# Two first-weight cells loaded whole, and the first ring load of the experts in four pieces

## The chip, the cores and the metric

The kernel runs on one core of one Trainium2 chip. The metric is the device time of one execution in microseconds. The profiled execution also gives a span, from the first to the last instruction of the program. The engines are PE (TensorE matmuls; PEld are its weight loads), DVE (VectorE), ACT (ScalarE), POOL (GpSimd) and SP (SyncE, which here only issues DMA transfers and waits; "SPq" in the rows). L927 means line 927 of the kernel before.

## The reference, cut to what matters

Two transformer-like blocks run one after the other on x of shape (1, 256, 1024) in float32. The first has two kinds of attention and a gated feed-forward layer. The second has a retention branch, an RWKV-7 recurrence and a mixture of 32 experts, of which each token uses two:

```
def second_block(x, ...):
        ret = retention(...) ; rw = rwkv7_time_mix(...)
        h = h + concat([ret, rw]) @ w_out
        h = h + hier_moe(rms_norm_2(h, norm2_gain), ...)
    return rms_norm_2(h, final_norm_gain)
...
    def expert_block(args):
        xblk, e = args
        hdn = jax.nn.silu(xblk @ w_gate[e]) * (xblk @ w_up[e])
        return hdn @ w_down[e]
```

Each expert has three matrices (gate, up, down) of 2 MB, so the 32 experts are 192 MB (201 million bytes) of weights, each of which is read once.

## The kernel before, in words

**Order of the work.** The first block runs up to about 345 us, then the projections of the second block, the recurrence (roughly 480 to 530 us), its output projection (to 554 us), the router (to 563 us) and the experts to the end. TensorE's program is written out by hand up to the first group of experts; after that it is a loop.

**Experts.** The experts are taken in eight groups of four (EG = 4). A group's work is: gather the chosen tokens (line 1942), multiply by gate and up (line 1962: for m in gate, up; for half in 0, 1; for k in 0..3; for expert j in 0..3), silu and product, multiply by down (line 1990), scatter. Up to 32 tokens of an expert make 32 columns, and the four experts run side by side on TensorE. After the last k of a half, the matmul of each expert adds 1 to the semaphore pieces_read, so the sync queue knows which weights may be overwritten.

**The ring.** From the second group on, the weights go through eight slots of 2 MB (two places with four experts each) in the big SBUF tensor arena. load_set (line 913) waits for pieces_read and issues the 2 MB load of one expert's matrix into slot_of(place, j); its landing adds 16 to ring_in[place][j], for which TensorE waits.

**The first group's weights** cannot go through the ring: they are put, before the ring starts, wherever room comes free. There are 24 cells of 1 MB, each one half of a matrix, that is 2048 columns of 128 rows. The table CELL says which half (q = 0, 1 gate; 2, 3 up; 4, 5 down) of which expert lies in which place: (0..3, i) are pieces of arena, (NQ, 0) and (NQ, 1) lie in the spent constants cst, (NQ + 1, 0) in x, (NQ + 2, i) in smaller pieces of several tensors. first_load (line 927) issues a cell, in pieces if first_parts says so, each piece after the fill for which it is told to wait: a cell in the tuple SPACED goes as four quarters of 512 columns (256 KB), the others go whole. The fills are TensorE's results in PSUM, named by tuples: ("U", c, par), ("St", c) and ("Y", ...) are steps of the recurrence over four chunks c of 64 tokens. All loads of lines 927 and 913 are on the one queue of SP, in the order in which moe_stream writes them: an issue that waits holds up all that stand behind it. The matmuls of the recurrence that appear in the rows are lines 1671 (U), 1688 (U with the state), 1705 (St), 1715 and 1732 (Y).

**Around the change.** In the recurrence moe_stream issues (2, 2) in quarters, (NQ, 1) in quarters waiting for ("U",1,1), ("St",1), ("St",1), ("U",2,1), (3, 2) in quarters waiting for ("U",2,1), ("St",2), ("St",2), ("U",3,1), and then the third piece of (NQ + 2, 3). The last first cell is (NQ + 1, 0), into x, issued at 561.58. The first ring load is expert 6's gate matrix into slot_of(1, 2). That slot is the same memory as the cells (3, 0) and (3, 1), which hold the first half of gate for experts 2 and 3; its columns 0 to 2047 are the one and 2048 to 4095 the other. It goes out once pieces_read is 4, that is when the first half of the first group's gate has been multiplied. The next ring load waits for pieces_read 5, one expert into the second half.

Of the kernel before, what the change touches and what calls it, by code (L numbers as in the profile page):

```python
# [30 lines left out]
P = 128  # L31
# [26 lines left out]
EG = 4  # L58
# [10 lines left out]
NQ = 4  # L69
# [260 lines left out]
def build(nc, A, out):  # L330
# [13 lines left out]
    with ExitStack() as ctx:  # L344
# [3 lines left out]
        def sem(name):  # L348
            return ctx.enter_context(nc.semaphore(name))
# [144 lines left out]
        def slot_of(place, j):  # L494
            lo = 2 * QUAD * place + SLOT * j
            return arena[:, lo:lo + SLOT]
# [103 lines left out]
        pieces_read = sem("pieces_read")  # L600
# [3 lines left out]
        u_first = sem("u_first")  # L604
        y_first = sem("y_first")
        rows_spent = sem("rows_spent")
        y_squared = sem("y_squared")
        y_gained = sem("y_gained")
        centre_ready = sem("centre_ready")
# [11 lines left out]
        ring_in = [[sem(f"ring_in{n}_{j}") for j in range(EG)] for n in range(2)]  # L621
# [31 lines left out]
        for u in range(9):  # L653
            lo = 512 * u if u < 4 else (2048 if u == 4 else NQKV + 512 * (u - 5))
            n = 256 if u == 4 else 512
# [193 lines left out]
        moe_w = {"gate": A["w_gate_2"], "up": A["w_up_2"], "down": A["w_down_2"]}  # L849
# [1 line left out]
        ALLQ = NG * QUADS_PER_GROUP  # L851


        SPACED = ((2, 0), (2, 1), (2, 2), (NQ, 0), (NQ, 1), (3, 3), (3, 2))

        SETS = 2 * 3
        LAST = NG // 2 - 1
# [26 lines left out]
        def _(sp):  # L884
# [19 lines left out]
            def load_set(r, pair, s, read, js=range(EG)):  # L904

                gp, kind = s // 3, ("gate", "up", "down")[s % 3]
                e0 = pair * (2 * EG) + gp * EG
                w = moe_w[kind][e0:e0 + EG] if isinstance(e0, int) else moe_w[kind][bass.ds(e0, EG)]
                w = w.rearrange("j (p k) n -> p j (k n)", p=P)
                for j in js:  # L910
                    if read is not None:
                        sp.wait_ge(pieces_read, read[j] if isinstance(read, dict) else read + (j + 1))
                    nc.sync.dma_start(slot_of(s % 2, j), w[:, j, :]).then_inc(ring_in[s % 2][j], 16)
# [6 lines left out]
            def first_load(at, j, *steps, lo=0, hi=4):  # L920

                w, col = half_of(*held_in[at, j]), 0
                for n, part in enumerate(first_parts(at, j)):
                    if lo <= n < hi:
                        if steps:
                            wait_filled(sp, *steps[n])
                        nc.sync.dma_start(part, w[:, col:col + part.shape[1]]).then_inc(quad_in[at][j], 16)  # L927
                    col += part.shape[1]

            def moe_stream(r, first):  # L930
                if first:
# [8 lines left out]
                    first_load(3, 3, *inv(("G1", 0), ("G1", 1), ("G2", 0), ("G2", 1)))  # L940
                    sp.wait_ge(mixed_ready, 1)
                    first_load(2, 2, ("U", 0, 1), ("St", 0), ("St", 0), ("U", 1, 1))
                    first_load(NQ, 1, ("U", 1, 1), ("St", 1), ("St", 1), ("U", 2, 1))
                    first_load(3, 2, ("U", 2, 1), ("St", 2), ("St", 2), ("U", 3, 1))
                    first_load(NQ + 2, 3, lo=2, hi=3)
                    sp.wait_ge(mixed_ready, NT)
                    sp.wait_ge(u_first, NCH - 1)
# [24 lines left out]
                    sp.wait_ge(xn_ready, 2 * NT)  # L972
                    sp.wait_ge(scattered, 2 * NT)
                    first_load(NQ + 1, 0)
                    load_set(0, 0, 3, {2: 4, 0: 5}, (2, 0))
                    sp.wait_ge(pieces_read, 8 + 1)
                    nc.sync.dma_start(quad[EXTRA_AT[0]][EXTRA_AT[1]], half_of(*EXTRA)).then_inc(extra_in, 16)
                    load_set(0, 0, 3, {1: 6, 3: 12}, (1, 3))
# [86 lines left out]
        def _(pe):  # L1065
# [841 lines left out]
            def moe_group(r, pair, gp, final=False):  # L1907
# [41 lines left out]
                for m in range(2):  # L1949
                    for half in range(2):  # L1950
                        if m == 0 and half == 1:
                            if isinstance(n, int) and n == 0:
                                wait_emptied(pe, "count")
                            gather(2)
                            gather(3)
                        for k in range(4):
                            if m == 0 and (half, k) in GATHERED_AT:
                                pe.wait_ge(xg_ready, len(GATHERS) * n + GATHERED_AT.index((half, k)) + 1)
                            for j in range(EG):
                                if k == 0:  # L1960
                                    half_ready(m, half, j)
                                ins = mm(psum[32 * j:32 * j + 32, MB[4 + m], :], xg[:, 4 * half + k, 32 * j:32 * j + 32],  # L1962
                                         weights(m, half, j, 512 * k), start=half == 0 and k == 0,
                                         stop=half == 1 and k == 3, skip_group_check=True)
                                if k == 3:
                                    ins.then_inc(pieces_read, 1)
                pe.wait_ge(shares_ready, n + 1)
# [56 lines left out]
            def moe_round(r):  # L2024
                if isinstance(r, int):
                    moe_group(r, 0, 0)
                    pe.wait_ge(count_ready, 1)
                    rows_most.append(pe.value_load(cnt[0:1, 0:1], min_val=0, max_val=T))
                    with pe.Fori(0, NG // 2 - 1) as pair:
                        moe_group(r, pair, 1)  # L2030
                        moe_group(r, pair + 1, 0)
                else:
                    with pe.Fori(0, NG // 2) as pair:
                        for gp in range(2):
                            moe_group(r, pair, gp)
# [1196 lines left out]
```

## Time and profile before

| | us |
|---|---|
| median of 3 runs | 1003.07 |
| lowest, highest | 1001.17, 1004.86 |
| the profiled execution | 1002.88 |
| its span | 1001.1 |
| PE busy, of the span | 873.7 |
| PEld, DVE, ACT busy | 603.4, 449.5, 331.9 |
| all DMA: moved, mean rate | 294.35 MB, 294 GB/s |

The page cuts the span into 40 slices of 25 us and gives the busy share of each engine in tenths (9 is 90% or more), the share of the 16 DMA engines, and the rate. The chain of waits follows the last instruction back to what released it, step by step. "issue" is time in which an engine waited for nothing that the profile shows. A DMA row gives the size of one transfer and the time from its issue to its landing.

### The profile page before, as it was taken

What the parts mean: (1) busy time and instruction counts of PE and PEld (TensorE: products, weight loads), DVE (VectorE), ACT (ScalarE), POOL (GpSimd) and SP (SyncE); (2) the same over time, 40 slices, a digit from 0 to 9 for tenths busy, and PEclk for the clock granted to TensorE, in tenths of its full rate; (3) what the DMA queues carried; (4) which work ended last, traced back from release to release, by engine and by line L of the source; (5) the groups of instructions that cost most, each with busy time, mean ns of one, the idle gap of its engine ahead of it and who ended that gap; (6) DMA issues with size and microseconds to landing.
All of it is one profiled execution on the core that took longest, in us unless ns stands there. A gap on an engine that the chain in (4) does not pass through costs nothing.

```text
span 1001.1 us, 16180 instructions
## 1 busy us (share of the span) xinstructions
PE 873.7 (87%) x6998; PEld 603.4 (60%) x6998; DVE 449.5 (45%) x586; ACT 331.9 (33%) x433; POOL 22.0 (2%) x35
## 2 busy tenths in 40 slices
PE   9999999999999999999989987767858776785785
PEld 8889988888888889989879632211312221131223
DVE  6776878688877438898766311000100000010002
ACT  6466664565555318745523300000000000000002
POOL 0420000000000000000100000000000000000000
PEclk9999999999999999999999999888977877788889
DMA  9893425576654536362459999999999999999995
GB/s 317 258 349 136 156 86 168 169 248 195 208 186 169 210 132 240 111 221 98 124 164 388 387 419 420 429 427 428 429 428 428 428 427 429 429 429 429 423 425 215
DMA packets 76113, 294.35 MB, mean 294 GB/s; under 512 B 5263, under 2 KB 32671, under 8 KB 62736
## 3 DMA queue, kind: packets, MB, share of 16 engines
q1 hardware_dynamic: 70496, 283.91, 72.6%
q10 hardware_dynamic: 4128, 6.34, 1.8%
q0 software_dynamic: 1424, 3.16, 1.1%
q8 instruction: 50, 0.82, 0.3%
q14 instruction: 15, 0.12, 0.0%
HBM read 290.25 MB, written 4.10 MB: 294 GB/s over the span
## 4 chain that ended last, share of the span: by engine, by line
PE 64%; DMA 28%; DVE 5%; SPq 1%; issue 1%; ACT 1%; DVEq 0%; ACTq 0%
DMA arena<-in_w_up 11%; DMA arena<-in_w_gate 9%; PE psum L1272 8%; DMA arena<-in_w_down 8%; PE psum L1962 7%; PE psum L1135 6%; PE psum L1137 6%; PE psum L1136 6%; PE psum L1299 4%; PE psum L1274 4%; PE psum L1990 3%; PE psum L1636 2%; PE psum L1172 1%; PE psum L1171 1%; PE psum L1169 1%; PE psum L1093 1%
## 5 line engine op out<-in xcount | busy, mean ns | idle before, releaser
L1962 PE MATMUL psum<-arena,featL 128*32 128x512 f32 x1008 | 161.8, 703 | 57.7 <-DMA arena<-in_w_up 39.1
L2545 DVE TENSOR_TENSOR ring_rounded<-arena,hi_rounded 128x2048 fp32r<-128x2048 f32 x75 | 171.4, 2289 | 60.6 <-ACT hi_rounded L2089 59.4
L2089 ACT ACTIVATE hi_rounded<-arena 128x2048 fp32r<-128x2048 f32 x76 | 144.8, 1911 | 84.6 <-DMA arena<-in_w_down 18.3
L1962 PEld LDWEIGHTS psum<-arena,featL 128*32 128x32 f32 x1008 | 38.1, 125 | 168.1 <-issue 85.1
L1272 PE MATMUL psum<-ffn_in_rounded,hi_rounded 128*128 128x512 f32 x352 | 122.4, 394 | 0.7 <-DVE ffn_in_rounded L2537 0.7
L1990 PE MATMUL psum<-arena,featT 128*32 128x512 f32 x424 | 76.7, 729 | 38.1 <-DMA arena<-in_w_down 33.7
L1135 PE MATMUL psum<-hi_rounded,featT_rounded 128*128 128x256 f32 (+1 forms) x336 | 104.1, 310 | 0.8 <-DVE ring_rounded L2545 0.7
L1137 PE MATMUL psum<-hi_rounded,featL_rounded 128*128 128x256 f32 (+1 forms) x336 | 101.8, 303 | 0.0
L1136 PE MATMUL psum<-ring_rounded,featT_rounded 128*128 128x256 f32 (+1 forms) x336 | 101.8, 303 | 0.0
L1274 PE MATMUL psum<-ffn_in_rounded,ring_rounded 128*128 128x256 f32 x352 | 97.5, 277 | 0.0
L1272 PEld LDWEIGHTS psum<-ffn_in_rounded,hi_rounded 128*128 128x128 f32 x352 | 66.0, 187 | 16.1 <-DVE ffn_in_rounded L2537 1.0
L3118 DVE TENSOR_TENSOR featT<-featT,psum 128x512 f32<-128x512 f32 x8 | 8.2, 1031 | 149.3 <-PE psum L1962 149.3
L1990 PEld LDWEIGHTS psum<-arena,featT 128*32 128x32 f32 x424 | 16.8, 130 | 88.8 <-DMA arena<-in_w_down 46.8
L1135 PEld LDWEIGHTS psum<-hi_rounded,featT_rounded 128*128 128x128 f32 x336 | 64.0, 191 | 4.5 <-issue 0.9
L1274 PEld LDWEIGHTS psum<-ffn_in_rounded,ring_rounded 128*128 128x128 f32 x352 | 66.1, 188 | 0.0
L1137 PEld LDWEIGHTS psum<-hi_rounded,featL_rounded 128*128 128x128 f32 x336 | 64.1, 191 | 2.6
L1136 PEld LDWEIGHTS psum<-ring_rounded,featT_rounded 128*128 128x128 f32 x336 | 64.1, 191 | 2.4
L3103 DVE TENSOR_TENSOR featL<-psum,gain 128x256 f32<-128x256 f32 x32 | 13.6, 425 | 104.4 <-PE psum L1942 104.4
L2448 ACT ACTIVATE featT<-psum 128x512 f32<-128x512 f32 x8 | 4.8, 598 | 162.2 <-PE psum L1962 162.2
L3131 DVE COPY featL<-psum 128x512 f32<-128x512 f32 x7 | 4.8, 692 | 119.1 <-PE psum L1990 119.1
L2450 ACT ACTIVATE featT<-psum 128x512 f32<-128x512 f32 x8 | 4.8, 597 | 132.8 <-PE psum L1978 132.8
L1942 PEld LDWEIGHTS psum<-featT,xn 128*128 128x128 f32 x256 | 32.0, 201 | 16.6 <-issue 14.0
(369 smaller groups left out, 1282.7 us busy)
## 6 DMA issues: line engine op xcount, KB each, us to landing
arena<-in_w_down SPq DMA_DIRECT2D x32, 2048.0 KB, 17.9
arena<-in_w_gate SPq DMA_DIRECT2D x28, 2048.0 KB, 20.7
arena<-in_w_up SPq DMA_DIRECT2D x24, 2048.0 KB, 23.3
arena<-in_w_in SPq DMA_DIRECT2D x14, 2048.0 KB, 9.0
arena<-in_w_up SPq DMA_DIRECT2D x25, 1024.0 KB, 8.8
arena<-in_w_gate SPq DMA_DIRECT2D x14, 1024.0 KB, 5.4
arena<-in_w_down SPq DMA_DIRECT2D x7, 1024.0 KB, 10.2
arena<-in_w_out SPq DMA_DIRECT2D x3, 2048.0 KB, 8.1
```

What stands on the lines that cost most here:

```text
L1135: mm(o, lhs[0], rhs[0], start=start, stop=False, skip_group_check=True)
L1136: mm(o, lhs[0], rhs[1], start=False, stop=False, skip_group_check=True)
L1137: return mm(o, lhs[1], rhs[0], start=False, stop=stop, skip_group_check=True)
L1272: mm(banks[f].rearrange("p (s t) -> p s t", s=2), hi_cols(g, k, P * f, P), ffn_both[:, :, k, :], start=k == 0, stop=k == DK - 1, skip_grou ...
L1274: ins = mm(banks[f][:, 0:T], lo_cols(g, k, P * f, P), ffn_parts[0][:, k, :], start=False, stop=k == DK - 1, skip_group_check=True)
L1299: return mm(b[:, f, :], w(g, k, P * f, P), r[:, k, :], start=(f, k) == (0, 0) and w is hi_cols and r is featR, stop=stop, skip_group_check ...
L1636: ins = mm(b[r, i, :], lhs[r, t, i, :], right, start=True, stop=True)
L1942: ins = mm(b[:, k - ks[0], :], xn[:, t, k * P:(k + 1) * P], G[:, t].rearrange("p e s -> p (e s)"), start=t == 0, stop=t == NT - 1)
L1962: ins = mm(psum[32 * j:32 * j + 32, MB[4 + m], :], xg[:, 4 * half + k, 32 * j:32 * j + 32], weights(m, half, j, 512 * k), start=half == 0 ...
L1990: return mm(psum[32 * j:32 * j + 32, MB[4 + half], :], hhT[:, k, 32 * j:32 * j + 32], weights(2, k // 2, j, at_), start=k == 0, stop=k == ...
L2089: fn(high, view, ACT.Copy).then_inc(hi_ready, 1)
L2545: tt(low, view, high.bitcast(F32), ALU.subtract).then_inc(lo_ready, 1)
```

## The change

Two cells leave SPACED and so are issued whole: (NQ, 1) with one wait for ("St", 1), and (3, 2) with one wait for ("U", 2, 1). The first load into the ring, 2 MB into slot_of(1, 2), becomes four loads of 1024 columns (512 KB): the columns of the k steps 0 and 1 of both cells after the matmul (m, half, k, j) = (0, 0, 1, 3), which now adds 1 to a new semaphore first_rows_read; the rest after pieces_read 4 as before. Three of the four add to a new semaphore second_gate_in, the last to ring_in[1][2] as the whole load did. TensorE waits for second_gate_in 48 once, after the first group and ahead of the loop over the others.

```diff
-        SPACED = ((2, 0), (2, 1), (2, 2), (NQ, 0), (NQ, 1), (3, 3), (3, 2))
+        SPACED = ((2, 0), (2, 1), (2, 2), (NQ, 0), (3, 3))
...
-                    first_load(NQ, 1, ("U", 1, 1), ("St", 1), ("St", 1), ("U", 2, 1))
-                    first_load(3, 2, ("U", 2, 1), ("St", 2), ("St", 2), ("U", 3, 1))
+                    first_load(NQ, 1, ("St", 1))
+                    first_load(3, 2, ("U", 2, 1))
...
-                    load_set(0, 0, 3, {2: 4, 0: 5}, (2, 0))
+                    w, at_ = moe_w["gate"][EG + 2].rearrange("(p k) n -> p (k n)", p=P), slot_of(1, 2)
+                    sp.wait_ge(first_rows_read, 1)
+                    for lo in (0, 2048):
+                        nc.sync.dma_start(at_[:, lo:lo + 1024], w[:, lo:lo + 1024]).then_inc(second_gate_in, 16)
+                    sp.wait_ge(pieces_read, 4)
+                    for lo, landed in ((1024, second_gate_in), (3072, ring_in[1][2])):
+                        nc.sync.dma_start(at_[:, lo:lo + 1024], w[:, lo:lo + 1024]).then_inc(landed, 16)
+                    load_set(0, 0, 3, {0: 5}, (0,))
...
+                                if first and (m, half, k, j) == (0, 0, 1, EG - 1):
+                                    ins.then_inc(first_rows_read, 1)
...
+                    pe.wait_ge(second_gate_in, 48)
```

## Rows read from the trace of the kernel before

**Rows 1.** The page's slices of 25 us: TensorE, DMA share, rate.
```profile
PE   9999999999999999999989987767858776785785
...
DMA  9893425576654536362459999999999999999995
GB/s 317 258 349 136 156 86 168 169 248 195 208 186 169 210 132 240 111 221 98 124 164 388 387 419 420 429 427 428 429 428 428 428 427 429 429 429 429 423 425 215
```

**Rows 2.** The chain that ended last: start us, us, what.
```profile
583.62 7.13 PE psum L1990 x64
590.75 24.36 DMA arena<-in_w_up
...
939.80 29.72 DMA arena<-in_w_up
969.57 4.63 PE psum L1962 x25
```

**Rows 3.** Single DMA issues at 561.58, 568.77, 574.20, 577.63: KB, us to landing.
```profile
x<-in_w_down SPq DMA_DIRECT2D x1, 1024.0 KB, 10.2
...
arena<-in_w_gate SPq DMA_DIRECT2D x1, 2048.0 KB, 9.3
...
arena<-in_w_gate SPq DMA_DIRECT2D x1, 2048.0 KB, 8.8
...
arena<-in_w_down SPq DMA_DIRECT2D x1, 1024.0 KB, 7.8
```

**Rows 4.** Busy time in windows; the last two columns are DMA share, GB/s.
```profile
568.00:574.00 6.00, 6.00 (x56) 2.93 (x52) 0.85 (x2) 0.00 (x0) 0.00 (x0) 1.00 0.96 360
574.00:578.00 4.00, 4.00 (x44) 1.30 (x40) 0.00 (x0) 0.60 (x1) 0.56 (x1) 1.00 0.98 360
```

**Rows 5.** The sync queue's waits, 560 to 585: us in total, times, longest.
```profile
SPq L913 <- PE psum L1962: 14.3, 3, 6.9
```

**Rows 6.** Timeline of TensorE in the first half: start, us.
```profile
564.99 3.64 PE L1962 MATMUL psum<-arena,featL 128*32 128x512 f32 x32
...
566.31 0.13 PEld L1962 LDWEIGHTS psum<-arena,featL 128*32 128x32 f32 x4 [0.30 <-issue]
```

**Rows 7.** Single DMA issues at 541.55, 547.81, 554.01, 554.38: KB, us to landing.
```profile
arena<-in_w_up SPq DMA_DIRECT2D x1, 1024.0 KB, 8.0
...
arena<-in_w_up SPq DMA_DIRECT2D x1, 1024.0 KB, 6.7
...
featL<-in_w_gate SPq DMA_DIRECT2D x1, 512.0 KB, 4.6
...
featT<-in_w_gate SPq DMA_DIRECT2D x1, 512.0 KB, 5.6
```

**Rows 8.** The DMA issue at 514.05: KB, us to landing.
```profile
arena<-in_w_gate SPq DMA_DIRECT2D x1, 256.0 KB, 2.8
```

**Rows 9.** Timeline of the sync queue, the eight quarters of the change: start, us.
```profile
519.04 3.74 SPq L927 DMA_DIRECT2D cst<-in_w_down  x4
522.83 2.97 SPq L927 DMA_DIRECT2D arena<-in_w_up  x4
```

**Rows 10.** DMA issues of 519 to 526.5: KB, median us to landing.
```profile
cst<-in_w_down SPq DMA_DIRECT2D x4, 256.0 KB, 4.0
```

**Rows 11.** Busy time in windows, quarters and whole cells; columns as above.
```profile
522.00:528.00 6.00, 6.00 (x160) 5.70 (x155) 3.84 (x9) 1.91 (x6) 0.00 (x0) 1.00 0.88 303
532.00:554.00 22.00, 21.94 (x182) 21.50 (x181) 10.06 (x11) 5.78 (x11) 0.00 (x0) 1.00 1.01 420
```

**Rows 12.** DMA of the instruction queue in 513.5:514.5 and 524:527: packets, MB, share.
```profile
q8 instruction: 1, 0.02, 7.4%
...
q8 instruction: 1, 0.02, 1.8%
```

**Rows 13.** Timeline of TensorE, 515 to 517: start, us, idle before.
```profile
514.83 0.68 PE L1705 MATMUL psum<-arena 128*64 128x64 f32 x15
516.30 0.22 PE L1705 MATMUL psum<-arena 128*64 128x64 f32 x1 [0.79 <-issue]
```

**Rows 14.** TensorE's waits, 530 to 565: us in total, times, longest.
```profile
PE psum L1834 <- DVE rt L3048: 0.7, 1, 0.7
```

More of the change, by code:

```diff
@@ L606, in build @@
         rows_spent = sem("rows_spent")
+        first_rows_read = sem("first_rows_read")
+        second_gate_in = sem("second_gate_in")
         y_squared = sem("y_squared")
```

## The prediction, made before the changed kernel ran

> **What bounds the kernel now.** I read the page's slices first [rows 1]. In the first two thirds TensorE is busy nearly all the time and the DMA engines are not. From slice 22 on it is the reverse: the DMA engines are full, at 419 and soon 427 to 429 GB/s. The chain that ended last [rows 2] shows how the two halves are joined. TensorE leads up to the middle of the first group of experts. Then transfers lead, one after another, up to the second halves of the last "up" weights, which were issued at 939.80 and land 29.72 us later, at 969.52. The tail, 31.6 us from there to the end of the span, opens with matmuls of the last group, and the change does not touch its work. So the end is (moment from which the transfers run without a gap) + (bytes left)/428 GB/s + a fixed tail of 31.6 us. Two things can move it: work of TensorE before the gapless stretch, and holes in the transfers ahead of it.
>
> Where does the gapless stretch begin? The single issues tell [rows 3]. The load into x, issued at 561.58, lands at 571.8 (10.2 us). The first ring load (2 MB), issued at 568.77, lands at 578.1 (9.3 us). The second, issued at 574.20, lands at 583.0 (8.8 us); the extra 1 MB, issued at 577.63, lands at 585.4 (7.8 us). A gapless 2 MB takes 2097 KB / 428 GB/s = 4.9 us, which is just the distance from 578.1 to 583.0, and 1 MB takes 2.45 us, the distance to 585.4. But from x at 571.8 to the first ring load are 6.3 us, 1.4 us too many. The rates agree [rows 4]: 360 GB/s from 568 to 578 where 428 would do, so (428 - 360)/428 = 16% of the time is missing, 0.95 us of it before 574 and 0.64 us after. This hole of about 1.5 us is what the second part of the change aims at. The sync queue is idle there: 14.3 us in three waits for the matmuls of line 1962 [rows 5].
>
> **Part 2, the first ring load in four.** Removed: one issue of 2 MB at 568.77. Added: two of 512 KB after the second k step (of four) of the first half, two after the last. The first half runs from 564.99 to 568.63 as 8 blocks of matmuls, one each 0.43 us, two to a k step; the fourth begins at 566.31 and its matmuls end about 0.6 us later [rows 6]. The old issue came 0.14 us after the last matmul, so the first pair goes out at about 567.05 and 567.4, the second at 568.77 and 569.15 (0.33 to 0.44 us each). x's load is still moving then, so the queue holds work throughout, and the 0.95 us before 574 should be closed. The small pieces carry a cost: two pieces of 512 KB issued at 554.01 and 554.38 landed 4.6 and 5.6 us later, at 558.6 and 560.0 [rows 7], 1.4 us apart where 1.23 would do. Four pieces: 4 x 0.2 = 0.8 us at most.
>
> The added wait of TensorE (second_gate_in, 48) comes after the first group, behind the matmuls of line 1990 that begin at 583.62 [rows 2]; what it waits for was needed by the next group anyway, and landed at 578.1. Nothing is queued behind it that was not waiting before. The added wait of the sync queue (first_rows_read) is met before the one that stood there (pieces_read 4), so nothing behind it gets later: the next issue, 574.20, waits for pieces_read 5.
>
> That issue is the cap. It is set by TensorE and is not moved. What would it land at on an empty queue? The quarter issued at 514, with nothing ahead of it, lands 2.8 us later [rows 8], 0.6 of them movement, so 2.2 are fixed. 574.20 + 2.2 + 4.9 = 581.3 instead of 583.0. **So no earlier loading alone can give more than 1.7 us, however much of it there is.** The lower bound is 0: the first hole is closed, the first ring load ends 0.95 us earlier, and the second hole (0.64 us now) grows by the same amount, since the next bytes arrive no sooner.
>
> **Part 1, two cells whole.** Removed: eight issues of 256 KB, from 519.04 to 525.8 [rows 9]. Added: two of 1 MB. The first waits for ("St", 1) as its second quarter did, the second for ("U", 2, 1) as its first did. The first group of four ends at 522.78, so its last quarter went at about 522.45, when ("U", 2, 1) was there: that is the second whole cell's time. The first lies between, at about 520.2. The last quarter of all went at 522.83 + 2.97 - 0.33 = 525.5, so the second cell is complete in the queue 3 us earlier. The piece into rows and the next whole cell follow at once, 3 us ahead too. Also, from 522 to 528, with quarters, the engines were at a share of 0.88 and 303 GB/s, and from 532 to 554, with whole cells, at 1.01 and 420 [rows 11]: per unit of busy time the quarters move 344, the whole cells 416.
>
> How much of this lead of up to 3.3 us is alive at 568? Every later load is issued on an event of TensorE, so a lead lives only while the queue has a backlog. A fresh 1 MB lands in 2.2 + 2.45 = 4.65 us. The load issued at 541.55 landed in 8.0, so 3.4 us of work lay ahead of it; the one at 547.81 landed in 6.7 (2.1 us ahead of it); the 512 KB at 554.01 in 4.6 against 3.4 fresh (1.2 us) [rows 7]. What exceeds 1.2 us is lost at 554 as idle transfer time. So part 1 brings 0 to 1.2 us, and the cap of 1.7 us holds for both parts together. On TensorE's own path it saves nothing: no first cell is waited for, since the chain goes over to transfers only at 590.75 [rows 2].
>
> **The sum.** Part 1 up to 1.2, part 2 up to 1.4 less up to 0.8 for the pieces, both together at most 1.7, at least 0. I take 1.1, a little over the middle, because the two parts each reach for the cap from another side. The profiled execution took 1002.88 us around a span of 1001.1; 1002.88 - 1.1 = 1001.8. It lies 0.2 below the median of the runs (1003.07), so the forecast is **1002.0 us**.
>
> **The rivals.** (a) *Given back wholly*, 1003.1 us: the ring's second load is all that counts, and it comes out at 583.0 as before. For it: its issue time does not move, and the window from 574 to 578 is short of bytes already. Against it: 583.0 is 1.7 us over what an empty queue would give.
>
> (b) *Slower through code loading*, 1004.4 us. TensorE's instructions come by DMA as well: the instruction queue moved one block of 0.02 MB between 513.5 and 514.5 [rows 12]. At 516.30 a matmul of line 1705 starts 0.79 us late with nothing in the profile to wait for [rows 13]. If the two belong together, TensorE can outrun its code in this stretch. Put a whole cell ahead of such a block and it waits for up to the 2.45 us of one cell instead of the 0.6 us of a quarter. The place is the block loaded between 524 and 527 [rows 12]; it decides once the block is late by more than TensorE's stock of code, which the trace does not show. Price from a gain (a block that happens to come sooner and saves a stop like that one, -0.79) to +2.45 us; this case takes 1003.07 - 1.1 + 2.45 = 1004.4. Against it: whole cells run from 532 on, and the list of TensorE's waits from 530 to 565 has no such stop, only one of 0.7 us for VectorE [rows 14]. The Trainium skill's "DMA: Bandwidth & Descriptors", section "Queues, rings and completion order", says that a DMA engine goes round the queues and empties a whole packet of descriptors, some 9 to 17, of one before it turns to the next. By that rule a whole cell could be one such packet per engine (an estimate: 128 rows over 16 engines are 8 descriptors), so that rule speaks for this rival and against the change; no row here shows a packet's bounds.
>
> (c) *The full cap*, 1003.07 - 1.7 = 1001.4 us: both holes close as far as the issue at 574.20 lets them. The Trainium skill's "DMA: Bandwidth & Descriptors", section "Measured (HBM→SBUF, 128 partitions, SWDGE, issued from GpSimd)", tells one to batch transfers to 1 MiB or more. It speaks for part 1 and against part 2. The trace charges small ones less than that where they overlap: the quarters of the first group land 4.0 us after issue (median) [rows 10], but four go out in 3.74 us [rows 9].
>
> (d) *It doesn't do what it says*: the first pair is not out before 568.8. Only if the sync queue were late; it has waited since its issue of 561.58, so 3 in 100.
>
> **Chances.** Forecast 0.50 (1001.5 to 1002.6), (a) 0.22, (b) 0.15, (c) 0.10, (d) 0.03. All lie within 1.7 us of before. A measurement of this kernel tells about 0.5% (5 us) from no change, and the three runs shown spread over 3.7 us. No mechanism here reaches 5 us: faster 0.03, same 0.93, slower 0.04. The range takes in (b) and (c) and most of the spread of the runs: 999.9 to 1004.7.
>
> **What would show it.** Right: two issues at 567.0 to 567.5; 400 GB/s and more from 568 to 574; the load issued at 574.2 lands 7.0 to 8.3 us later; from there to the end the same 418 us as before. For part 1: whole cells near 520 and 522.5, and landing times of the loads at 541.6 and 547.8 shorter by 1 to 3 us. Wrong: that second load lands 8.8 us after issue (a); TensorE's first matmul of line 1962 comes after 565.0 (b), with new stops without a releaser between 520 and 532. A difference of over 3 us would mean that TensorE's path before 565 has changed, which I do not expect.

## The result: slower by 0.2%, and the profile after

Over 20 runs each, the changed kernel takes 1005.38 us (median; 1002.61 to 1008.19) and the kernel before 1003.14 us (1000.34 to 1005.50). The ratio is 1.0021, with a 95% interval of 1.0014 to 1.0028: 2.2 us slower. That lies within the 0.5% that the prediction called "same", but outside its range (999.9 to 1004.7) and on the other side of its forecast of 1.1 us faster. The profiled execution took 1006.05 us, its span is 1004.2 (before 1002.88 and 1001.1).

In kernel.py of after, the lines behind the change have moved by 2 to 12: 927 is 929, 1093 is 1102, 1135 to 1137 are 1144 to 1146, 1688, 1705 and 1732 are 1697, 1714 and 1741, 1962 is 1971, 1990 is 2001, 2996 is 3008.

The page's slices of 25 us, to be read against [rows 1]: TensorE, its granted clock in tenths, DMA share, rate. The two slices from 525 to 575 us stand out: 349 and 366 GB/s where [rows 1] has 388 and 387:

```profile
PE   9999999999999999999988988767857776786785
...
PEclk9999999999999999999999998777978788788788
...
DMA  9893324576645546452468999999999999999995
GB/s 328 250 356 139 139 87 167 168 252 210 205 168 185 193 160 218 136 200 85 130 188 349 366 413 424 429 427 427 428 429 428 428 428 428 429 429 429 423 424 223
```

The chain that ended last, the same steps as [rows 2] (start, us, what). The step over to transfers comes at 594.61 in place of 590.75, 3.9 us later; the last "up" weights land at 943.73 + 27.81 = 971.54 in place of 969.52:

```profile
587.48 7.13 PE psum L2001 x64
594.61 24.07 DMA arena<-in_w_up
...
943.73 27.81 DMA arena<-in_w_up
971.58 5.55 PE psum L1971 x25
```

So the difference is made before the gapless stretch, as the frame of the prediction says; but it is made by TensorE. The place is at 526 us. Timeline of TensorE in after, matmuls and then the weight load ahead of them (start, us, idle before and its supposed releaser):

```profile
526.09 0.92 PE L1741 MATMUL psum<-arena,featT 128*64 128x64 f32 x13
530.29 1.08 PE L1102 MATMUL psum<-cst,xn 128*128 128x128 f32 x4 [3.28 <-DVE xn L3008]
...
530.26 0.71 PEld L1102 LDWEIGHTS psum<-cst,xn 128*128 128x128 f32 x4 [3.39 <-issue]
```

TensorE stands still for 3.3 us at the end of the recurrence. In before, the matmuls of line 1093 follow those of line 1732 at once. These are the steps of the chain there, first of after and then of before; after the stop the matmuls follow each other every 0.21 us, before every 0.12:

```profile
528.98 0.61 DVE xn L3008
529.59 0.70 issue
530.29 1.08 PE psum L1102 x4
531.37 0.21 PE psum L1144
```

```profile
526.16 1.83 PE psum L1732 x32
527.99 0.62 PE psum L1093 x4
528.61 0.12 PE psum L1135
```

The windows tell why (columns as in [rows 4]; the third last is the granted clock). First before, then after:

```profile
528.00:530.00 2.00, 2.00 (x17) 2.00 (x18) 1.69 (x5) 1.28 (x3) 0.00 (x0) 1.00 1.07 254
532.00:534.00 2.00, 2.00 (x19) 2.00 (x18) 0.82 (x2) 0.71 (x2) 0.00 (x0) 1.00 0.98 401
```

```profile
528.00:530.00 2.00, 0.00 (x0) 0.00 (x0) 1.30 (x3) 0.16 (x1) 0.00 (x0) 1.00 1.04 393
530.00:532.00 2.00, 1.71 (x8) 1.74 (x9) 0.00 (x0) 0.54 (x2) 0.00 (x0) 0.57 0.97 410
532.00:534.00 2.00, 2.00 (x13) 2.00 (x12) 1.80 (x4) 2.00 (x3) 0.00 (x0) 0.57 1.05 442
534.00:538.00 4.00, 4.00 (x37) 4.00 (x36) 0.61 (x2) 0.65 (x2) 0.00 (x0) 1.00 1.01 420
```

No matmul from 528 to 530, then a granted clock of 0.57 for four microseconds (the mean of a stretch at 1.2 GHz, 530.30 to 533.71, and the rest at 2.4), then 1.00 again.

What belongs to this stop is a block of TensorE's own code. The transfers of the instruction queue at 527.6 to 527.8 in after, and at 525.3 to 525.6 in before (packets, MB, share): the same block, 2.2 us later.

```profile
q8 instruction: 1, 0.02, 27.6%
```

```profile
q8 instruction: 1, 0.02, 18.3%
```

**Where the time went, from the two traces.** TensorE entered the last chain of the recurrence 0.98 us earlier in this execution of after (at 520.65, before at 521.63), which is scatter, since it arises ahead of the changed loads. From there to the issue of the ring's second load it took 57.40 us in place of 52.57: +4.83, that is 3.28 of stop and 1.55 that I put to the low clock. That load landed 7.7 us after its issue instead of 8.8 [rows 3]: -1.05. From its landing to that of the last "up" weights 385.8 in place of 386.6: -0.78. The tail 32.7 in place of 31.6: +1.1. Together -0.98 + 4.83 - 1.05 - 0.78 + 1.13 = 3.15, the difference of the spans.

### The profile page after: what moved, and what is told of

Same layout as the page of the kernel before. It is cut to its first block, busy times and chain, and to the rows that moved or that the text cites. A ratio compares the mean times of both kernels' runs of the same rounds, so it can differ in the third digit from the quotient of the medians.

```text
span 1004.2 us, 16177 instructions
## 1 busy us (share of the span) xinstructions
PE 875.4 (87%) x6998; PEld 605.3 (60%) x6998; DVE 449.5 (45%) x586; ACT 332.0 (33%) x433; POOL 21.9 (2%) x35
## 4 chain that ended last, share of the span: by engine, by line
PE 63%; DMA 28%; DVE 6%; issue 1%; SPq 1%; ACT 1%; DVEq 0%; ACTq 0%
DMA arena<-in_w_up 11%; DMA arena<-in_w_gate 9%; PE psum L1281 8%; DMA arena<-in_w_down 8%; PE psum L1971 8%; PE psum L1144 6%; PE psum L1146 6%; PE psum L1145 6%; PE psum L1308 4%; PE psum L1283 4%; PE psum L2001 4%; PE psum L1645 2%; PE psum L1181 1%; PE psum L1180 1%; PE psum L1178 1%; PE psum L1102 1%
## 5 line engine op out<-in xcount | busy, mean ns | idle before, releaser
L2001 PE MATMUL psum<-arena,featT 128*32 128x512 f32 x424 | 78.8, 740 | 36.1 <-DMA arena<-in_w_down 31.7
```

Of the source, the lines that this page charges most:

```text
L2001: return mm(psum[32 * j:32 * j + 32, MB[4 + half], :], hhT[:, k, 32 * j:32 * j + 32], weights(2, k // 2, j, at_), start=k == 0, stop=k == ...
```

## The experiments

All are compared at the same four places, since single executions differ by 2 us and more in their total. TensorE's instructions (matmuls, weight loads, and the waits and register operations of its sequencer) are numbered in order of start. "Delay" is the time from TensorE's entry into the block of 256 ahead of the one in question (instruction 9153) to the start of the transfer of the next one (instructions 9409 and on). The request itself is not in the trace; the entry stands for it. For a later block (9921) the transfer began 0.5 to 0.8 us ahead of the entry in the four runs with a low clock, so the entry is not exactly the request. "Stop" is the idle time that the timeline shows there, "way" is the time from TensorE's instruction 9075 to the issue of the ring's second load, less the 52.57 us of before, and "load" is that second load from issue to landing. In shift, where the way's first point does not compare, none is given.

| kernel | delay | stop | way | load | median (runs), ratio to before |
|---|---|---|---|---|---|
| before | 2.19 | none | 0 | 8.75 | 1003.14 (20) |
| after | 5.42 | 3.28 | +4.83 | 7.70 | 1005.38 (20), 1.0021 [1.0014, 1.0028] |
| after_b | 4.92 | 2.73 | +4.29 | 8.89 | 1006.12 (8), 1.0023 [1.0012, 1.0033] |
| part1 | 5.83 | 3.55 | +5.08 | 8.20 | 1004.56 (12), 1.001 [1.000, 1.002] |
| part2 | 1.89 | none | 0.00 | 8.49 | 1003.44 (12), 1.0002 [0.9993, 1.001] |
| burst | 3.07 | 1.08 | +1.11 | 7.91 | 1003.35 (12), 1.0002 [0.9989, 1.0015] |
| halves | 3.74 | 1.36 | +1.38 | 7.73 | 1005.71 (1) |
| only_nq1 | 2.00 | 0.54 | +0.56 | 10.09 | 1001.42 (1) |
| only_32 | 4.34 | 2.18 | +3.70 | 7.72 | 1004.42 (1) |
| late32 | 1.72 | none | +0.01 | 9.82 | 1003.66 (12), 1.0001 [0.9991, 1.0011] |
| shift | 4.67 | 1.49 | | 9.73 | 1003.44 (12), 1.0005 [0.9995, 1.0016] |
| allwhole | 3.82 | 1.63 | +1.66 | 8.85 | 1004.49 (10), 1.0013 [1.0002, 1.0025] |
| eighths | 1.73 | none | 0.00 | 9.91 | 1002.65 (10), 0.9989 [0.9976, 1.0002] |
| eighths_b | 2.10 | none | -0.01 | 7.82 | 1002.20 (12), 0.9991 [0.998, 1.0003] |

**Each part alone.** My theory was that part 1 delays a block of code and so stops TensorE; the rival, that the stop is a wait for data (the timeline names VectorE's line 3008), and that part 2 has its share.

part1 leaves the first ring load whole and changes only the recurrence:

```diff
-        SPACED = ((2, 0), (2, 1), (2, 2), (NQ, 0), (NQ, 1), (3, 3), (3, 2))
+        SPACED = ((2, 0), (2, 1), (2, 2), (NQ, 0), (3, 3))
...
-                    first_load(NQ, 1, ("U", 1, 1), ("St", 1), ("St", 1), ("U", 2, 1))
-                    first_load(3, 2, ("U", 2, 1), ("St", 2), ("St", 2), ("U", 3, 1))
+                    first_load(NQ, 1, ("St", 1))
+                    first_load(3, 2, ("U", 2, 1))
```

> The kernel before with part 1 alone (two cells whole, the ring's first load in one piece). Theory C (code): TensorE runs out of instructions, because the 256-instruction block it needs next waits in the DMA engines behind whole cells. It expects the stop of 3.3 us near 527 to be here too, the instruction queue's transfer 5 us and more after TensorE entered its last block, and a time of before + 3 to + 5 us (1006 to 1008). Rival D (data): the stop is a wait for VectorE's result (line 3008 of after), which the whole cells or the changed ring load delayed; it expects the stop too, but with VectorE's chain late on its own account. Rival R (ring): the stop belongs to the split of the ring load or to the shifted program; it expects no stop here and before's time.

part2 is the rest of the change, with both cells in quarters:

```diff
-                    load_set(0, 0, 3, {2: 4, 0: 5}, (2, 0))
+                    w, at_ = moe_w["gate"][EG + 2].rearrange("(p k) n -> p (k n)", p=P), slot_of(1, 2)
+                    sp.wait_ge(first_rows_read, 1)
+                    for lo in (0, 2048):
...
+                    sp.wait_ge(pieces_read, 4)
...
+                    load_set(0, 0, 3, {0: 5}, (0,))
```

> The kernel before with part 2 alone (first ring load in four, cells in quarters). Theory C expects no stop at 527, and the gain of the closed hole: second ring load landing 0.5 to 1.7 us earlier against its issue, time before - 0.5 to - 1.5 us (1001.6 to 1002.6). If the gain measured in after (the second ring load lands 7.7 us after its issue in place of 8.8) came from part 1's lead alone, this run lands at 8.8 and equals before.

Timeline of TensorE at the end of the recurrence, part1 and then part2:

```profile
531.02 0.98 PE L1093 MATMUL psum<-cst,xn 128*128 128x128 f32 x4 [3.55 <-DVE xn L2996]
```

```profile
526.94 0.66 PE L1102 MATMUL psum<-cst,xn 128*128 128x128 f32 x4
```

The whole stop and the whole low clock come with part 1. Part 2 costs nothing, but it brings nothing either, and its trace shows why. With TensorE on time, the first pair goes out at 566.00 and 566.37, the second at 567.80 and 568.17. x lands at 570.37 and the last piece at 575.63, 5.3 us later in place of 6.3: the first hole is closed by 1.0. But the second load, issued at 573.22, lands at 581.71, 6.1 us after the last piece in place of 4.9, and 8.5 us after its issue in place of 8.8. From x to the second load it is 11.3 us, in before 11.2. part1's median is 1.5 us over the 1003.04 of before on that chip, less than the 2.2 of after, though its trace shows no less on the way (+5.08) and the intervals overlap. Its profiled execution, 1007.43 us, is the longest of its 12, so its stop may be longer in the trace than in most of its runs; the difference is not explained.

Windows of part2, against [rows 4]: 345 where 360 stood, and 379 where 360 stood. The prediction's sign, 400 GB/s and more from 568 to 574, is not there.

```profile
568.00:574.00 6.00, 6.00 (x59) 2.89 (x61) 0.85 (x2) 0.60 (x1) 0.39 (x1) 1.00 0.97 345
574.00:578.00 4.00, 4.00 (x44) 1.19 (x39) 0.00 (x0) 0.00 (x0) 0.17 (x1) 1.00 1.00 379
```

**Moving the program under the block bounds.** If the stop belongs to the code, it must move when TensorE's program grows; if it belongs to data, it must stay at line 1102. part2 speaks against data already: its matmuls of line 1102 start at 526.94, while VectorE's line 3008 starts at 528.90, the same time as in after, so they don't wait for it. shift is the changed kernel with 19 idle matmuls at the start of TensorE's program turned into 51 of a smaller size (what they compute is not used). The trace counts each as two matmuls and two weight loads, so the 32 more make 128 instructions more:

```diff
-            idle(19)
+            for _ in range(19 + 32):
+                mm(psum[0:32, 7, 0:64], late[:, 0:32], late[:, 0:64], start=True, stop=True)
```

> The changed kernel, with TensorE's program made 128 instructions longer at its start: the 19 idle matmuls of line 1112 become 51 narrower ones, so each block of 256 instructions ends half a block earlier in the program. Everything else is as in after. Theory C expects the stop at 527 to vanish (the block boundary is 128 instructions earlier, entered before the whole cells are in the queue, and the next falls into slow code after 529), stops elsewhere of up to 1 us, and a time 2 to 4 us below after, at 1001.5 to 1003. Rival D (a data wait) expects the same 3.3 us stop at the same matmul and after's 1005.4.

```profile
524.96 0.28 PE L1725 MATMUL psum<-xn,arena 64*64 64x64 f32 x2
526.72 0.97 PE L1725 MATMUL psum<-xn,arena 64*64 64x64 f32 x30 [1.49 <-issue]
```

The stop left line 1102 and stands in the midst of a group of 32 equal matmuls of line 1725, two of which ran before it. No data can part these. It stands at instruction 9409 again. I had expected it to vanish; it shrank to 1.5 us, since this block runs 5.8 us and not 4.5 before the next is due. The median, 1003.44, is a little over the 1001.5 to 1003 expected and some 2 us under that of after. The rival is refuted; the name of VectorE at this stop was only the last event before it (the weight load of the same moment says "issue").

**Row size against time of issue.** burst issues the quarters at the moments of the whole cells: same bytes, same moments, 2 KB rows for 8 KB. halves does it with 4 KB rows.

```diff
-                    first_load(NQ, 1, ("U", 1, 1), ("St", 1), ("St", 1), ("U", 2, 1))
-                    first_load(3, 2, ("U", 2, 1), ("St", 2), ("St", 2), ("U", 3, 1))
+                    first_load(NQ, 1, *[("St", 1)] * 4)
+                    first_load(3, 2, *[("U", 2, 1)] * 4)
```

> Part 1 alone but in pieces: both cells go as four quarters each, all four at the moment at which the whole cell went. Same bytes at the same time, rows of 2 KB in place of 8 KB. If the late code block is a matter of row size (a block gets its turn only after a long run of 8 KB rows), the stop near 527 is gone or below 1 us, time within 1 us of before. If it is a matter of how many bytes stand ahead, the stop is 2.5 to 3.5 us as in after, time before + 3 to + 4 us. Rival D expects what part 1 alone shows.

```diff
+            if (at, i) in ((NQ, 1), (3, 2)):
+                return [quad[at][i][:, 1024 * n:1024 * n + 1024] for n in range(2)]
...
+                    first_load(NQ, 1, *[("St", 1)] * 2)
+                    first_load(3, 2, *[("U", 2, 1)] * 2)
```

> Part 1 alone in two pieces of 512 KB for each cell, both at the moment of the whole cell: rows of 4 KB, between the 2 KB of the run in quarters at one moment (stop 1.2 us, block 3.1 us after the request) and the 8 KB of part 1 (stop 3.7 us, block 5.8 us). If the block waits behind a number of rows that is the same in all three, its delay grows with the row: about 4.0 us after the request and a stop of about 2 us. If pieces are what counts (each new transfer gives the code a turn), 2 pieces give a block at 4.5 us and more, stop 2.5 to 3 us; if bytes alone, 5.8 and 3.7.

TensorE at the end of the recurrence, burst and then halves:

```profile
529.23 0.63 PE L1093 MATMUL psum<-cst,xn 128*128 128x128 f32 x4 [1.08 <-issue]
```

```profile
530.72 0.63 PE L1095 MATMUL psum<-cst,xn 128*128 128x128 f32 x4 [1.36 <-ACT arena L2399]
```

The delay of the block is 2.19 with quarters spread out, 3.07 with the same quarters at once, 3.74 with halves at once, 4.92 to 5.83 with whole cells at once. So both count: the bytes queued ahead (0.9 us) and the size of the pieces (1.9 to 2.8 us from quarter to whole). I had expected one or the other. burst and halves are one trace each, and after and after_b, one program, differ by 0.5: the order fits, the single steps are not shown to that size. For part 1's effect on the transfers, the loads of after at 545.40, 551.65 and 557.85 (the ones of 541.55, 547.81 and 554.01 in [rows 7]) and then those of burst (542.79, 549.06, 555.26), each with its time to landing:

```profile
arena<-in_w_up SPq DMA_DIRECT2D x1, 1024.0 KB, 5.3
...
arena<-in_w_up SPq DMA_DIRECT2D x1, 1024.0 KB, 5.0
...
featL<-in_w_gate SPq DMA_DIRECT2D x1, 512.0 KB, 3.9
```

```profile
arena<-in_w_up SPq DMA_DIRECT2D x1, 1024.0 KB, 6.7
...
arena<-in_w_up SPq DMA_DIRECT2D x1, 1024.0 KB, 5.4
...
featL<-in_w_gate SPq DMA_DIRECT2D x1, 512.0 KB, 4.3
```

Shorter by 2.7, 1.7 and 0.7 us in after, by 1.3, 1.3 and 0.3 in burst. But most of this is no lead: TensorE, stopped, issues these loads 4.8 us later in after and 1.1 us later in burst. Counted from its instruction 9075, the first of the three lands after 28.0 us in before, 30.0 in after, 27.7 in burst and 27.6 in halves; the third after 36.9, 41.1, 37.8 and 37.9. So a lead of the transfers shows only in burst and halves, as 0.3 us, and it is gone by the third load.

**Which cell.** only_nq1 makes (NQ, 1) whole and leaves (3, 2) in quarters; only_32 the reverse. late32 is the changed kernel with the whole (3, 2) held until ("U", 3, 1).

```diff
-        SPACED = ((2, 0), (2, 1), (2, 2), (NQ, 0), (NQ, 1), (3, 3), (3, 2))
+        SPACED = ((2, 0), (2, 1), (2, 2), (NQ, 0), (3, 3), (3, 2))
...
+                    first_load(NQ, 1, ("St", 1))
```

> The kernel before with the cell (NQ, 1) alone whole, at ("St", 1), some 3 us ahead of the moment (523.3 in the trace of before) when TensorE enters its last stocked block. Theory C expects the code block to come as before (about 2.2 us after TensorE enters the block ahead of it) or up to 1 us later, and a stop near 527 of 0 to 0.5 us.

```diff
-        SPACED = ((2, 0), (2, 1), (2, 2), (NQ, 0), (NQ, 1), (3, 3), (3, 2))
+        SPACED = ((2, 0), (2, 1), (2, 2), (NQ, 0), (NQ, 1), (3, 3))
...
+                    first_load(3, 2, ("U", 2, 1))
```

> The kernel before with the cell (3, 2) alone whole, at ("U", 2, 1), and what follows it in the queue 3 us earlier. It stands in the queue just as TensorE asks for the next code block. Theory C expects the block 4 to 6 us after the request in place of 2.2, and most of part 1's stop: 2 to 3.5 us.

```diff
-                    first_load(3, 2, ("U", 2, 1))
+                    first_load(3, 2, ("U", 3, 1))
```

> The changed kernel, with the whole cell (3, 2) held back until ("U", 3, 1), 3 us later, as late as its last quarter went in before. The code block asked for at about 522.3 then has only (NQ, 1) ahead of it. Theory C expects no stop above 0.5 us at the block's end near 527, the second ring load landing 7.7 to 8.5 us after its issue, and a time of 1002 to 1003, that is 2 to 3 us below after. Rival D expects after's 1005.4.

only_nq1, only_32 and late32 at the end of the recurrence:

```profile
527.89 0.63 PE L1093 MATMUL psum<-cst,xn 128*128 128x128 f32 x4 [0.54 <-issue]
```

```profile
529.59 0.63 PE L1093 MATMUL psum<-cst,xn 128*128 128x128 f32 x4 [2.18 <-issue]
```

```profile
527.61 0.66 PE L1102 MATMUL psum<-cst,xn 128*128 128x128 f32 x4
```

It is what is freshly queued when TensorE enters the block (at 522.3 to 523.0): (3, 2) and, just behind it, the next whole cell (2, 3), which a whole (3, 2) lets go out 4 us earlier too (in after at 522.4; before at 526.8). (NQ, 1), issued three microseconds before that entry, delays hardly. One wait moved in late32 takes the stop away. It does not bring the forecast gain: its second load lands 9.8 us after issue, and its ratio to before is 1.0001. only_32 also shows the clock by itself, from 530 to 536; the level of 0.50 is 1.2 GHz:

```profile
530.00:532.00 2.00, 2.00 (x15) 2.00 (x13) 0.98 (x3) 1.69 (x3) 0.00 (x0) 0.70 1.02 430
532.00:534.00 2.00, 2.00 (x12) 2.00 (x11) 1.29 (x2) 0.90 (x1) 0.00 (x0) 0.50 1.05 434
534.00:536.00 2.00, 2.00 (x18) 2.00 (x18) 0.00 (x0) 0.00 (x0) 0.00 (x0) 0.94 0.98 406
```

**More and fewer whole cells.** allwhole is the kernel before with all seven cells of SPACED whole, each behind the last of its four waits; eighths has them in eight pieces with 1 KB rows, two to a wait.

```diff
-        SPACED = ((2, 0), (2, 1), (2, 2), (NQ, 0), (NQ, 1), (3, 3), (3, 2))
+        SPACED = ()
...
-                            wait_filled(sp, *steps[n])
+                            for step in steps if at != NQ + 2 else steps[n:n + 1]:
+                                wait_filled(sp, *step)
```

> The kernel before with all seven cells of SPACED issued whole, each after the last of the four steps that its quarters waited for (so no byte starts earlier). Theory code behind fresh whole cells: a block of 256 TensorE instructions (0.02 MB) that is asked for while such a cell has just been queued comes 5.4 us after its request instead of 1.3 to 2.4 us; between 485 and 530 us TensorE enters a new block every 3.3 to 5 us, so each of the five other cells that meets a request should cost a stop of 1 to 3.5 us with no releaser, at TensorE instruction numbers 256 apart, and those above 2 us a lower granted clock behind them. Sum: three to six stops, TensorE 5 to 15 us later at the second ring load, median 1008 to 1018. Rival, only that one place is tight (something particular to the stretch at 527): +3 us as in part1, median 1004.5 to 1006, no new stops from 485 to 515.

```profile
494.74 0.35 PE L1584 MATMUL psum<-arena 64*64 64x64 f32 x9 [1.67 <-issue]
...
528.89 0.63 PE L1094 MATMUL psum<-cst,xn 128*128 128x128 f32 x4 [1.63 <-ACT arena L2398]
```

Two stops and not three to six. The one near 495 had been 0.6 us and grew to 1.7; the one at 529 is new; but the two of before near 512 and 516 went. The times of issue tell why. The two whole cells ahead of a stop went out 1.6 and 0.75 us before TensorE entered a block (488.19 and 489.75; 521.80 and 522.55), and the next block's transfer began 2.6 and 3.8 us after that entry. The other five went out 0.4 to 2.4 us after such an entry; around four of them the block's transfer began after 1.0 to 1.8 us, and the fifth, (3, 2) at 524.79, came when the late block was due already. The first expectation counted cells, and cells do not count: only what has just been queued when a block is asked for. The median, 1004.49, is the one that the rival gave (1004.5 to 1006) and not 1008 to 1018.

```diff
-            return [quad[at][i][:, 512 * n:512 * n + 512] for n in range(4)] if (at, i) in SPACED else [quad[at][i]]
+            return [quad[at][i][:, 256 * n:256 * n + 256] for n in range(8)] if (at, i) in SPACED else [quad[at][i]]
...
-                            wait_filled(sp, *steps[n])
+                            wait_filled(sp, *steps[n if at == NQ + 2 else n // 2])
```

> The kernel before with the seven cells of SPACED as eight pieces of 256 columns (128 KB, rows of 1 KB) in place of four of 512, two pieces per step waited for, so the same bytes at the same moments. Theory, the delay of a code block goes with the row size (3.1, 3.7, 5.4 us measured for rows of 2, 4 and 8 KB): with 1 KB it is under 2.5 us everywhere, and the three stops of the kernel before (0.79, 0.58 and 1.01 us at the block ends near 497, 514 and 518) shrink to below 0.3 each: TensorE up to 2 us earlier, median 1001 to 1003, if the shorter rows do not cost as much in the transfers. Rival, the delay goes with the bytes queued in a burst and not with the row: the stops stay at 0.6 to 1.0, median 1003 to 1004.

> The same kernel as eighths, timed again over more rounds, to settle whether the 0.8 us by which its median lay below the kernel before is real. Theory code blocks: two of the three stops of the kernel before (0.58 and 1.01 us) are gone again, the one near 497 stays at 1.3, TensorE about 1 us earlier at the second ring load; that load still lands 8 to 10 us after issue, so the ratio is 0.9985 to 0.9995. Rival, the gain is taken back by the ring's transfers: ratio 1.0000 with TensorE just as early.

Two of the three stops that these expectations name, 0.58 and 1.01 us, are no stops for code: at 506.57 and 521.74 of before TensorE waits for VectorE (instructions 8312 and 9077, not a multiple of 256 from the others), and both waits stay in eighths (0.85 and 1.02) and in eighths_b. Those for code in before are 0.57 us at 494.48, 0.36 at 512.12 and 0.79 at 516.30. In eighths the stops near 512 and 516 were gone and the one near 494 was 1.1 us in place of 0.6. In eighths_b, the same program, the one before 516 stood again:

```profile
515.79 0.22 PE L1705 MATMUL psum<-arena 128*64 128x64 f32 x1 [1.12 <-issue]
```

So rows of 1 KB are no cure, and the size of the row is not all that makes such a block late: with the same 1 KB rows, this block's transfer began 0.97 us after TensorE entered the block ahead in eighths and 2.12 us after it in eighths_b (1.77 in before, with 2 KB). Both medians are about 1 us under before (0.8 and 1.2), both intervals just include 1. Taken together they speak for a gain of one in a thousand; that it is real isn't shown, and its cause is open.

**The changed kernel once more.** after_b is the changed kernel, unaltered.

> The changed kernel once more, unaltered, for a second trace and more times. The first trace puts the start of the gapless transfers 2.8 us later than in before although TensorE's path was 1 us ahead of before's up to 520, so the trace alone speaks for + 3.8 us, while the medians differ by 2.2. If the stop at the block's end is the same each time, it is 3.3 to 3.5 us here too, and the difference of the medians stays between 1.5 and 4. If it varies from execution to execution, it is clearly shorter or longer here.

The stop is 2.73 us with the clock low again, the ratio 1.0023. Its trace has a second difference, 1.5 us in place of 0.4 at line 1667 at 513.66; halves has the same (at 513.49). The transfer of that block began 3.3 us after the entry ahead of it in these two and 1.0 to 2.2 us in the others, and both stops lie ahead of the changed loads: the blocks of code come late by themselves too.

## Why the prediction was wrong, point by point

**The frame was right.** The end is the second ring load's landing plus a constant: from there to the last "up" landing it is 384.6 to 387.4 us in all 14 traces.

**The step that failed** is the last of part 1: "On TensorE's own path it saves nothing". It costs 3.3 us of stop and 1.5 us of low clock there. What happened is rival (b), at the place it named: the block loaded between 524 and 527, behind whole cells. The prediction gave it 15 in 100, for two reasons, and both were wrong.

*"It decides once the block is late by more than TensorE's stock of code, which the trace does not show."* The trace did show it. The three stops without a releaser, 0.79 us in [rows 13] and two like it, each stand at a multiple of 256 instructions from one another (7617, 8641, 8897), and at each a block had landed 1.2 to 1.4 us before TensorE went on, so there was no stock. The account for the block at 9409 can be made up from before: TensorE takes 4.5 us for the 256 instructions ahead of it; the block is moved 2.19 us after TensorE enters these, in 0.9 us; with 1.2 to 1.4 us until TensorE goes on that is 4.3 to 4.5. So at most 0.2 us were to spare, and beyond that **every microsecond of delay is a microsecond of stop.** At 9409 itself TensorE goes on 1.4 to 1.7 us after the block is there (after 528.57 and 530.29, allwhole 527.22 and 528.89); I take 1.5, which is fitted to these runs. With each run's delay and 0.9 + 1.5 - 4.5 this gives 3.3 for after, 3.7 for part1, 2.2 for only_32, 1.6 for halves, 1.7 for allwhole, 0 for late32, part2 and eighths, against 3.28, 3.55, 2.18, 1.36, 1.63 and none. (burst 1.0 against 1.08; in only_nq1 the block was moved in 1.7 us and not in 0.9.)

The Trainium skill's "Runtime: NRT & Kernel Launch", section "Instruction fetch mechanics", says that code comes in blocks of 256 instructions over a DMA queue of the sequencer's own, the next while the current one runs, and that this is mostly hidden. The blocks agree with the trace (0.02 MB, stops at multiples of 256); "mostly hidden" holds from 528 on, where a block lasts 12.6 to 15.4 us, and not for the recurrence, where it lasts 3.2 to 7.0 us.

*"Against it: whole cells run from 532 on, and the list of TensorE's waits has no such stop."* True [rows 14], but no evidence. TensorE takes 15.4 us for the block that it enters at 527.88, where the one before took 4.5. The transfer of its successor began 4.5 us after that entry in before, 6.1 in part2 and 6.6 in only_nq1, with three whole cells issued from 1.1 us before it to 0.3 us after it, and nothing showed. The cover was in the code, not in the transfers.

**The price was too low.** Its upper bound of 2.45 us was one cell's time. In the run two whole cells and a piece stood in the queue, and the block was 3.2 us later than before. One whole cell can be harmless (late32, issued 3.2 us before the entry: delay 1.72) or not (allwhole, issued 0.75 us before it, with an older one in flight and another issued 2.2 us after it: 3.82). The prediction quotes a rule of the Trainium skill, "DMA: Bandwidth & Descriptors", section "Queues, rings and completion order", by which at most one packet of the other queue would be waited for, by its estimate one cell, 2.45 us. The 1.6 and 2.15 us by which the block was later than before in allwhole and only_32 fit that; the 3.2, 2.7 and 3.6 us of after, after_b and part1 are more. And the stop had a second price that no rival held: after stops of 1.1 to 1.6 us the clock stayed at 1.00 and the way grew by the stop alone (1.08 and 1.11, 1.36 and 1.38, 1.63 and 1.66); after stops of 2.2 to 3.6 us it fell, and the way grew by 1.5 us more in each of the four runs (2.18 and 3.70, 2.73 and 4.29, 3.28 and 4.83, 3.55 and 5.08).

**Part 2** went as rival (a) had it: the first hole closed by 1.0 and the second grew by 1.2. The sum took 1.1 "because the two parts each reach for the cap from another side"; no part reached it with certainty. The second load's times from issue to landing, 7.7 to 10.1 us over the runs, scatter more than the 1.1 us to be found.

**Part 1's lead** came out at its low end: the prediction took up to 1.2 us at 554, and the runs in which a lead can be read (burst, halves) show 0.3 us for the loads of 541 and 547 and none at 554. Its sign, landing times shorter by 1 to 3 us, came true for another reason, the lateness of TensorE. In after the second load landed 1.05 us sooner after its issue than in before, as it might with TensorE late and the queue not; but after_b, with the same stop, has 8.89 against 8.75, so this is not shown to be more than scatter. **The cap** of 7.1 us from issue to landing held in all runs (lowest 7.70).

## What to carry to other kernels

Before large transfers are moved into a stretch in which TensorE runs many short matmuls, make up the account of its code: where stops without a releaser stand 256 instructions apart, there is no stock, and the free time is the time that 256 instructions take, less delay, move and restart of a block. There, put large transfers behind the start of a block's transfer rather than just ahead of it; one wait moved did that here. It took away the loss and won nothing over the kernel before. And a stretch in which large transfers do no harm proves nothing for another in which the same number of instructions takes a third of the time.

## What had not been expected of the hardware

- The delay of a code block depends on what was queued just before: for the one at 9409 it is 1.9 to 2.2 us among spaced quarters, 3.1, 3.7 and 4.9 to 5.8 among 2, 4 and 8 KB rows of both cells queued at once. Others vary by themselves: the one at 8641 took 3.3 us in after_b and halves and 1.4 to 2.2 in before and in the seven other runs that have the same loads and the same code ahead of it. In the full queue from 542 on it was still only 2.1 in before, so a full queue is not enough; why fresh whole cells are worse than old ones is open.
- After each of the four stops of 2.18 to 3.55 us the granted clock was 0.50 (1.2 GHz) for 3.4 us, and the way grew by 1.5 us beyond the stop. After the stops of 0.54 to 1.63 us at the same place in other runs it stayed at 1.00.
- The timeline's releaser of such a stop is whatever ended last: VectorE's line 3008 (2996 in the numbering of before), ScalarE's 2399 and "issue" were named for the same stop in after, part1, halves and burst.
